# Opening of a two-block transformer kernel: x loaded ahead of the vectors, side loads behind it, zeros multiplied while TensorE waits

## The reference, cut to what matters

```python
def ada_mod(c, w, b, n):
    h = jax.nn.silu(c) @ w + b
    return jnp.split(h[:, None, :], n, axis=-1)

def gmlp_layer(x, c, ada_w, ada_b, norm_g, w_in, sgu_g, w_s, b_s, w_out):
    shift, scale, gate = ada_mod(c, ada_w, ada_b, 3)
    h = rms_norm(x, norm_g) * (1 + scale) + shift
    u, v, z = jnp.split(h @ w_in, 3, axis=-1)
    u = jax.nn.gelu(u)
    v = rms_norm(jax.nn.gelu(v), sgu_g)
    w_causal = jnp.tril(w_s)
    mixed = jnp.einsum('gts,bcsge->bctge', w_causal, v) + b_s
    y = u * mixed.reshape(bsz, s, A_WIDTH) * jax.nn.silu(z)
    return x + gate * (y @ w_out)
```

## Time and profile before

| | value |
|---|---|
| median of 3 runs | 1493.45 us (1486.89 to 1493.67) |
| the profiled execution | 1486.86 us |
| its span, first to last instruction | 1485.1 us |
| mean granted TensorE clock, share of full | 0.996 |
| TensorE busy | 1447.9 us, 97% |
| VectorE busy | 953.3 us, 64% |
| ScalarE busy | 624.3 us, 42% |
| DMA moved | 181.06 MB, 122 GB/s over the span |

### The profile page before, as it was taken

One profiled execution on the slowest core, in us unless ns is written; L12 is line 12 of the kernel. 1 busy time (PEld: TensorE's weight loads), 2 busy tenths in 40 slices (PEclk: granted clock), 3 DMA queues, 4 the chain that ended last, 5 costly groups with the idle time before them and its releaser, 6 DMA issues.

```text
span 1485.1 us, 19595 instructions
## 1 busy us (share of the span) xinstructions
PE 1447.9 (97%) x7404; PEld 1183.0 (80%) x7404; DVE 953.3 (64%) x1392; ACT 624.3 (42%) x916; POOL 124.8 (8%) x58
## 2 busy tenths in 40 slices
PE   5999999999999999999999999999899999999999
PEld 3998888888788688888877787777488888888887
DVE  5975777777888466666666868779777344332333
ACT  4734223332466444444444456655555232211221
POOL 0000100001100322222212100000020000000000
PEclk9999999999999999999999999999999999999999
DMA  9785544467622111111111232012021322222222
GB/s 378 302 344 201 185 183 170 169 242 284 265 75 86 61 63 51 56 55 56 57 57 57 85 115 86 29 60 84 1 102 70 113 85 103 95 98 101 85 92 78
DMA packets 34269, 181.06 MB, mean 122 GB/s; under 512 B 3865, under 2 KB 4121, under 8 KB 19618
## 3 DMA queue, kind: packets, MB, share of 16 engines
q1 hardware_dynamic: 32114, 175.22, 32.0%
q10 hardware_dynamic: 2096, 5.04, 1.0%
HBM read 178.14 MB, written 2.11 MB: 121 GB/s over the span
## 4 chain that ended last, share of the span: by engine, by line
PE 87%; DVE 6%; DMA 4%; issue 1%; ACT 1%; SPq 0%; ACTq 0%; DVEq 0%
PE acc L1519 75%; PE ada L1519 4%; PE norm L1519 4%; DMA ada_out<-in_ada 3%; PE turn L1519 2%; PE turn L1754 1%; DVE w_lo L915 1%; PE turn L1873 1%; DVE hx L908 1%; DMA wf_raw<-in_forget 1%; DVE hk_lo L908 0%; DVE s L908 0%; DVE ada_out L908 0%; DVE h_lo L908 0%; DVE stat L1373 0%
## 5 line engine op out<-in xcount | busy, mean ns | idle before, releaser
L1519 PE MATMUL acc<-h_hi,w_hi 128*128 128x512 f32 x984 | 400.8, 407 | 0.0
L1519 PE MATMUL acc<-h_hi,w_lo 128*128 128x512 f32 x984 | 383.8, 390 | 0.0
L1519 PE MATMUL acc<-h_lo,w_hi 128*128 128x512 f32 x984 | 383.5, 390 | 0.0
L915 DVE TENSOR_TENSOR w_lo<-w_raw,w_hi 128x2048 fp32r<-128x2048 f32 (+1 forms) x89 | 205.9, 2314 | 69.0 <-ACT w_hi L491 68.8
L491 ACT ACTIVATE w_hi<-w_raw 128x2048 fp32r<-128x2048 f32 (+1 forms) x106 | 200.7, 1893 | 117.1 <-PE acc L1519 117.0
L1519 PEld LDWEIGHTS acc<-h_hi,w_hi 128*128 128x128 f32 x984 | 184.9, 188 | 46.1 <-issue 9.0
L1519 PEld LDWEIGHTS acc<-h_lo,w_hi 128*128 128x128 f32 x984 | 185.0, 188 | 44.6 <-issue 8.1
L1519 PEld LDWEIGHTS acc<-h_hi,w_lo 128*128 128x128 f32 x984 | 184.7, 188 | 39.1
L445 POOL TENSOR_TENSOR w_lo<-w_raw,w_hi 128x2048 fp32r<-128x2048 f32 x17 | 77.3, 4548 | 322.4 <-ACT w_hi L491 322.4
L1519 PE MATMUL acc<-w_hi,h_hi 128*128 128x256 f32 x320 | 92.6, 289 | 0.0
L1519 PE MATMUL acc<-w_lo,h_hi 128*128 128x256 f32 x320 | 90.5, 283 | 0.0
(11 more groups left out here) (256 smaller groups left out, 2574.7 us busy)
## 6 DMA issues: line engine op xcount, KB each, us to landing
w_raw<-in_weights SPq DMA_DIRECT2D x102, 1024.0 KB, 4.7
ada_v<-in_ada SPq DMA_DIRECT2D x32, 512.0 KB, 5.9
ada_raw<-in_ada SPq DMA_DIRECT2D x32, 512.0 KB, 6.0
ada_out<-in_ada SPq DMA_DIRECT2D x32, 512.0 KB, 6.4
ada_up<-in_ada_first SPq DMA_DIRECT2D x8, 1024.0 KB, 20.2
w_raw<-in_weights SPq DMA_DIRECT2D x4, 768.0 KB, 4.2
x<-in_x SPq DMA_DIRECT2D x2, 1024.0 KB, 9.4
w_first<-in_weights SPq DMA_DIRECT2D x2, 1024.0 KB, 16.3
```

What stands on the lines that cost most here:

```text
L915: nc.vector.tensor_tensor(w_lo[par][:, 0:used], w_raw[par][:, 0:used], f32(w_hi[par][:, 0:used]), ALU.subtract)\
L1519: return nc.tensor.matmul(out, lhsT, rhs, start=start, stop=stop)
```

## The change

- SP issues the two halves of x right after c, and `vecs` behind them.
- The constants are laid out anew so that the matrix of ones and the epsilon are the first 132 columns. ACT issues just these first (`ones_loaded`). `csil[1]`, the rest of `consts`, and `ws_t` are issued in the loop over the tiles, after `h_hi` of tile 6; `lam_rows`, `bf_col`, `wf_raw` and `b_sp` after the loop.
- The load of the logarithm table moves from before the eight squares to behind them.
- DVE adds the squares in pairs (0+1, 2+3, 4+5, 6+7), ahead of the six gains, and TensorE adds the four sums with four products into `norm`.
- TensorE multiplies zeros into the bank `ada`: 6 products of 128 x 512 after spreading c, 16 after the sum of the squares. POOL clears the tile of zeros.
- `lam` moves: its two sums on DVE come after the masking of `ws_t`, behind a wait for all four small loads; its exponential on ACT after the statistics of v; `neg_lam` on DVE after them too. The wait for `small_loaded` ahead of the next stage goes.
- The third chunk's first group of tokens takes its 16 products with `h_hi` first and the 8 with `h_lo` behind them, one tile at a time as `h_lo` gets ready (`rows_late`). The wait for all of `h_lo` ahead of `v_pair(1)` goes, and `v_pair(1)` is taken out of the loop.

```diff
-    tiles = [ident, ones, half, causal_t, np.where(d >= 0, d, FAR), np.where(i >= j, 0.0, -FAR), slopes, last]
+    tiles = [ones, last, ident, half, causal_t, np.where(d >= 0, d, FAR), np.where(i >= j, 0.0, -FAR), slopes]
...
+    idle = at("idle", [P, TOK], T[7], F32R)
...
             sp.dma_start(c_in[:, :], d["c"]).then_inc(c_loaded, 16)
-            sp.dma_start(vecs[:, :], d["vecs"]).then_inc(vecs_loaded, 16)
             for half in range(2):
                 sp.dma_start(x[:, 4 * half:4 * half + 4, :], d["x"][:, 4 * half:4 * half + 4, :]).then_inc(x_loaded[half], 16)
+            sp.dma_start(vecs[:, :], d["vecs"]).then_inc(vecs_loaded, 16)
...
             nc.gpsimd.memset(one_row[:, :], 1.0).then_inc(one_ready, 1)
+            nc.gpsimd.memset(idle[:, :].bitcast(F32), 0.0).then_inc(idle_ready, 1)
...
-            act.dma_start(consts[:, :], d["tiles"]).then_inc(consts_loaded, 16)
-            act.dma_start(lam_rows[:, :], d["diff_lam_2"][0].rearrange("a b -> (a b)").partition_broadcast(P)).then_inc(small_loaded, 16)
-            act.dma_start(bf_col[:, :], d["b_f_2"].rearrange("a h -> h a")).then_inc(small_loaded, 16)
-            act.dma_start(wf_raw[:, :, :], d["forget"]).then_inc(small_loaded, 16)
-
-            act.dma_start(csil[1][:, :], d["c_2"][0].partition_broadcast(P)).then_inc(c2_loaded, 16)
+            act.dma_start(consts[:, 0:K_ID], d["tiles"][:, 0:K_ID]).then_inc(ones_loaded, 16)
...
-            act.preload_act_table_set("natural_log_exp_and_others")
             for kt in range(KT):
                 act.wait_ge(x_loaded[kt // 4], 16)
                 nc.scalar.activation(sq_first[kt][:, :], x[:, kt, :], ACT.Square).then_inc(sq_ready, 1)
+            act.preload_act_table_set("natural_log_exp_and_others")
             rstd_start(N_X0, NB[:, :], DM)
-            act.wait_ge(lam_part, 2)
-            nc.scalar.activation(lam_two[:, :], lam_two[:, :], ACT.Exp).then_inc(lam_exp, 1)
...
                 nc.scalar.activation(h_hi[:, kt, :], h_full[:, kt, :], ACT.Copy).then_inc(hhi_done, 1)
-
-            act.dma_start(ws_t[:, :, :], d["spatial"]).then_inc(ws_loaded, 16)
+                if kt == KT - 2:
+                    act.dma_start(csil[1][:, :], d["c_2"][0].partition_broadcast(P)).then_inc(c2_loaded, 16)
+                    act.dma_start(consts[:, K_ID:NCONST], d["tiles"][:, K_ID:NCONST]).then_inc(consts_loaded, 16)
+                    act.dma_start(ws_t[:, :, :], d["spatial"]).then_inc(ws_loaded, 16)
+
+            act.dma_start(lam_rows[:, :], d["diff_lam_2"][0].rearrange("a b -> (a b)").partition_broadcast(P)).then_inc(small_loaded, 16)
+            act.dma_start(bf_col[:, :], d["b_f_2"].rearrange("a h -> h a")).then_inc(small_loaded, 16)
+            act.dma_start(wf_raw[:, :, :], d["forget"]).then_inc(small_loaded, 16)
...
+            for i in range(KT // 2):
+                dve.wait_ge(sq_ready, 2 * i + 2)
+                nc.vector.tensor_tensor(sq_first[2 * i][:, :], sq_first[2 * i][:, :], sq_first[2 * i + 1][:, :], ALU.add)\
+                    .then_inc(sq_added, 1 + i // 2)
...
-            dve.wait_ge(small_loaded, 48)
-            for n in range(2):
-                stt(lam_prod[:, 64 * n:64 * n + 64], lam_rows[:, 128 * n:128 * n + 64], 1.0,
-                    lam_rows[:, 128 * n + 64:128 * n + 128], ALU.mult, ALU.mult, accum_out=lam_two[:, n:n + 1]).then_inc(lam_part, 1)
-            for m in range(1, KT - 1):
-                dve.wait_ge(sq_ready, m + 1)
-                if m > 1:
-                    dve.wait_ge(sq_added, m - 1)
-                nc.vector.tensor_tensor(sq_first[0][:, :], sq_first[0][:, :], sq_first[m][:, :], ALU.add).then_inc(sq_added, 1)
...
             nc.vector.tensor_tensor(ws_t[:, :, :], ws_t[:, :, :], tri, ALU.mult).then_inc(ws_ready, 1)
+            dve.wait_ge(small_loaded, 64)
+            for n in range(2):
+                stt(lam_prod[:, 64 * n:64 * n + 64], lam_rows[:, 128 * n:128 * n + 64], 1.0,
+                    lam_rows[:, 128 * n + 64:128 * n + 128], ALU.mult, ALU.mult, accum_out=lam_two[:, n:n + 1]).then_inc(lam_part, 1)
...
+            def stay_busy(n):
+                for _ in range(n):
+                    mm(AD[:, :], idle[:, 0:P], idle[:, :], True, True)
+
...
-            pe.wait_ge(consts_loaded, 16)
-            pe.wait_ge(sq_added, KT - 2)
-            mm(NB[:, :], ones, sq_first[0][:, :], True, False)
-            pe.wait_ge(sq_ready, KT)
-            mm(NB[:, :], ones, sq_first[KT - 1][:, :], False, True).then_inc(sum_done, 1)
+            pe.wait_ge(idle_ready, 1)
+            stay_busy(6)
+            pe.wait_ge(ones_loaded, 16)
+            for i in range(KT // 2):
+                pe.wait_ge(sq_added, (1, 2, 4, 6)[i])
+                last = mm(NB[:, :], ones, sq_first[2 * i][:, :], i == 0, i == KT // 2 - 1)
+            last.then_inc(sum_done, 1)
+            stay_busy(16)
...
+                            if first and (par, hb, t) == (0, 0, 0):
+                                last = rows_late(G[0][:, 0:256], 0, 0, 256)
...
-            h_ready(0, KT - 1)
-            with pe.Fori(1, W_UZ // 2) as u:
+            def rows_late(out, par, t, n):
+
+                wh = w_hi[par][:, :].rearrange("p (k n) -> p k n", k=KT)
+                wl = w_lo[par][:, :].rearrange("p (k n) -> p k n", k=KT)
+                s = slice(P * t, P * t + P)
+                for kt in range(KT):
+                    mm(out, h_hi[:, kt, s], wh[:, kt, 0:n], kt == 0, False)
+                    mm(out, h_hi[:, kt, s], wl[:, kt, 0:n], False, False)
+                for kt in range(KT):
+                    h_ready(0, kt)
+                    last = mm(out, h_lo[:, kt, s], wh[:, kt, 0:n], False, kt == KT - 1)
+                return last
+
+            v_pair(1, True)
+            with pe.Fori(2, W_UZ // 2) as u:
                 v_pair(u)
```

More of the change, by code:

```diff
@@ L100, in constants @@
     last = np.broadcast_to(np.array([EPS, 0.0, 0.0, 0.0]), (P, 4))
-    tiles = [ident, ones, half, causal_t, np.where(d >= 0, d, FAR), np.where(i >= j, 0.0, -FAR), slopes, last]
+    tiles = [ones, last, ident, half, causal_t, np.where(d >= 0, d, FAR), np.where(i >= j, 0.0, -FAR), slopes]
     return [np.concatenate(part, axis=1).astype(np.float32) for part in (tiles, blocks)]
-K_ID, K_ONE, K_HALF, K_TRI, K_DIST, K_MASK = 0, P, 2 * P, 3 * P, 4 * P, 4 * P + TOK
+K_ONE, K_EPS, K_ID = 0, P, P + 4
+K_HALF, K_TRI, K_DIST = K_ID + P, K_ID + 2 * P, K_ID + 3 * P
+K_MASK = K_DIST + TOK
 K_SLOPE = K_MASK + P
-K_EPS = K_SLOPE + 24
-NCONST = K_EPS + 4
+NCONST = K_SLOPE + 24
 def program(nc, d):
@@ L251, in sem @@
         return nc.alloc_semaphore(name)
-    vecs_loaded, consts_loaded, ws_loaded = sem("vecs_loaded"), sem("consts_loaded"), sem("ws_loaded")
+    vecs_loaded, ones_loaded, consts_loaded, ws_loaded = sem("vecs_loaded"), sem("ones_loaded"), sem("consts_loaded"), sem("ws_loaded")
     x_loaded = [sem("x_loaded0"), sem("x_loaded1")]
@@ L263, in program @@
     up_done, up_out, gsa_done = sem("up_done"), sem("up_out"), sem("gsa_done")
-    xn_done, one_ready = sem("xn_done"), sem("one_ready")
+    xn_done, one_ready, idle_ready = sem("xn_done"), sem("one_ready"), sem("idle_ready")
     hi_done, lo_done = sem("hi_done"), sem("lo_done")
@@ L597, in _ @@
             nc.scalar.activation(v_stat[:, 3, :], v_stat[:, 2, :], ACT.Square, scale=math.sqrt(0.5 / AW)).then_inc(v_stat_act, 1)
+            act.wait_ge(lam_part, 2)
+            nc.scalar.activation(lam_two[:, :], lam_two[:, :], ACT.Exp).then_inc(lam_exp, 1)
             def uz_pair(u):
@@ L1076, in _ @@
                 nc.vector.tensor_tensor(h_lo[:, kt, :], h_full[:, kt, :], f32(h_hi[:, kt, :]), ALU.subtract).then_inc(hlo_done, 1)
-            dve.wait_ge(lam_exp, 1)
-            stt(neg_lam[:, :], lam_two[:, 1:2], -LAM_INIT, lam_two[:, 0:1], ALU.add, ALU.subtract).then_inc(lam_ready, 1)
             ada_v_units(0, 0)
@@ L1101, in _ @@
             stt(v_stat[:, 5, :], v_stat[:, 4, :], 1.5, v_stat[:, 2, :], ALU.subtract, ALU.mult, reverse0=True).then_inc(v_stat_dve, 1)
+            dve.wait_ge(lam_exp, 1)
+            stt(neg_lam[:, :], lam_two[:, 1:2], -LAM_INIT, lam_two[:, 0:1], ALU.add, ALU.subtract).then_inc(lam_ready, 1)
             def uz_pair(u, cond):
@@ L1126, in uz_pair @@
                                             ALU.subtract).then_inc(ylo_done, 1)
-            dve.wait_ge(small_loaded, 64)
             half_uz = W_UZ // 2 + (C2_UNIT - FIRST_UZ_UNIT) // (2 * UNITS_UZ)
@@ L1603, in _, with v_pair @@
                 mm(G[n][:, :], one_row[:, :], c_in[:, TOK * n:TOK * n + TOK], True, True).then_inc(c_spread_in, 1)
-            pe.wait_ge(consts_loaded, 16)
-            pe.wait_ge(sq_added, KT - 2)
-            mm(NB[:, :], ones, sq_first[0][:, :], True, False)
-            pe.wait_ge(sq_ready, KT)
-            mm(NB[:, :], ones, sq_first[KT - 1][:, :], False, True).then_inc(sum_done, 1)
-            def v_pair(u):
-                n = 2 * u - W_V
+            pe.wait_ge(idle_ready, 1)
```

(7 more changed lines are left out.)

## The result

The changed kernel takes 1481.78 us (median of 20 runs, 1478.32 to 1486.60) against 1490.15 (20 runs of the kernel before, 1486.27 to 1493.67). The ratio is 0.9946, 95% interval 0.9936 to 0.9957: 8.0 us less, between 6.4 and 9.5. The profiled execution took 1483.68 us, its span is 1481.9. The forecast was 1484, with 6.3 us less.

What follows compares the result with a forecast made beforehand. TensorE was taken as the bound (87% of the chain), so it must start earlier or wait less: third chunk 6.7 us earlier, less 0.4 at chunk (2,0), gives 6.3; 1490.2 - 6.3 = 1483.9, predicted 1484 us, range 1476 to 1491.

Steps and rivals of the forecast that it cites:

- x and the bytes ahead: Opening loads: with a start of 3.4 us at 418 GB/s, x's halves land at 6.1 and 8.6 us.
- The norm: Opening, after the squares: the last pair is added by 11.95 us and its product ends at 12.9.
- The second `ada_up` is late next: DVE's `up_unit(1)` waits for this load behind 6.5 MB; DVE's series moves from 24.93 to 19.2, 5.7 us earlier.
- TensorE waits behind tile 0: First chunks: tile 0 ends at 21.7 at full rate, tile 1 comes at 22.9, so TensorE waits 1.2 us.
- Issues on ACT's path: ACT after tile 6: three DMA issues cost 1.35 us, later ones about 1.4; third chunk starts at 48.5.
- Low halves last: Third chunk: `h_lo` ends at 50.3, needed at 50.4; `rows_late` avoids a wait of 1.8 us, leaving none or 0.2.
- Chunk (2,0): Two chunks after the third chunk's start: its slack of 1.1 us is overdrawn by 0.3 to 0.4 us.
- The gain stays: Stages after chunk (2,0): TensorE or loads released by its own progress set the pace, so 6.3 us remains.
- E: Rival, later stages: the gain gets lost in a stage that loads pace; time 1486.9 us; chance 0.10.
- B: Rival, opening: products of zeros don't raise TensorE's clock; gain 4.0 us, time 1482.9; chance 0.15.
- D: Rival, DVE's wait for four small loads: late `b_sp` makes it slower, 1491 us if landing at 75; chance 0.05.
- C: Rival, opening: small loads and issues cost nothing, `ada_up` in time; gain about 8 us, time 1478.8; chance 0.15.

Runs made afterwards that it cites:

- side loads in front: Changed kernel with `csil[1]`, the rest of `consts`, `lam_rows`, `bf_col` and `wf_raw` issued at the start again, behind the ones; ratio 0.9980 to the kernel before.
- zeros alone: Kernel before with only the 22 products of zeros added; ratio 1.0002 to the kernel before.
- six zeros: Changed kernel without the 16 products of zeros behind the norm, keeping the 6 ahead of it; ratio 0.9952 to the kernel before.
- loads only: Changed kernel without any products of zeros and with the old third chunk, waiting for all eight `h_lo`; ratio 0.9967 to the kernel before.
- wait for all low halves: Changed kernel with the wait for all eight `h_lo` ahead of the third chunk and the old product order; ratio 0.9966 to the kernel before.

## Why the prediction was right, and where it was off

The time (1484 for 1481.78) and the sign came out; the size was a little too small (6.3 us, just below the interval of 6.4 to 9.5 around 8.0). Part of this is luck. The level that 6.3 was taken from, 1490.2, was the middle between two pairs of runs, a guess, and the median of before came out at 1490.15. And two misses partly cancel: the third chunk began 8.1 us earlier and not 6.7, and 1.0 us of it was lost ahead of chunk (2,0) and not 0.4. By its steps:

- *x and the bytes ahead.* Squares ran unbroken from 6.59 to 11.04; the sum had 6.8 to 11.2. The start of 3.4 us was the right end. Its reason is not shown: with the side loads in front again the second `ada_up`, behind 7.7 MB, fits a start of about 4.9 us, although the stretch at 116 GB/s isn't there.
- *The norm.* Ended at 13.4, not 12.9: its first products ran at half rate (1.06 to 1.08 each) and only those from 11 on at full rate (0.59). Harmless, since the load was later.
- *The second `ada_up` is late next.* Landed at 18.99, `up_unit(1)` at 19.01; the sum said 19.2 and not the 17.9 of the norm alone. (That 17.9 was 0.3 too late: `up_unit(1)` began 4.74 us behind the end of the norm, at 24.93 for 20.19, which from 12.9 gives 17.6. It bound nothing.) With 1.2 MB more in front it was 23.35, where the same sum would say 22.1.
- *TensorE waits behind tile 0.* 0.4 us instead of 1.2, as tile 0 began later (18.6) and tile 1 came sooner (22.7).
- *Issues on ACT's path.* This term was mis-sized. Three issues were priced at 1.35 us and kept ACT idle for 0.73 and DVE, ahead of `to_lo(1, 0)`, for 0.97; four at the end were priced to bring the table to 46.2 to 46.6, and it was loaded at 44.99. The step that was off is the sum of issue times: the first issue behind an activation runs beside it. So bank G[0] was empty in time and the third chunk began at 47.09 instead of 48.5.
- *Low halves last.* They ended at 49.5 (50.3 said), and there was no wait. Undone, the wait is 2.7 us, not 1.8, as TensorE is free at 47.0 and not at 48.5, and the cost at chunk (2,0) is 2.9: the clock that falls in the wait was left out.
- *Chunk (2,0).* The overdrawn slack was there: 0.8 us of waiting where 0.3 to 0.4 were said, larger because TensorE was earlier. The 0.38 us for `lam` fell into the wait for `ada_v`, still 1.12 us long behind them.
- *The gain stays.* 7.17 us at 84.50 and the same at 316.27. E fell; that the profiled spans differ by less is the clock, since TensorE's later waits are the same.
- *B*, zeros that give no clock, fell by the run with zeros alone and the one with six. The rule cited from the Trainium skill, "TensorE: Matmul & The Clock Gate" (The HAM clock gate), that activity releases the throttle, agrees with the traces for zeros as well: 0.67 and 0.59 a pair at 1.00 granted, against 1.19 at 0.50 without them. With the zeros alone the stretch from 18 to 22 us is at 0.50 and that from 24 to 26 at 1.00, and from 22 to 24, where the clock rose, TensorE multiplied nothing but zeros.
- *D.* `small_loaded` held nobody: `lam_prod` ran at 62.3, straight behind the masking.
- *C* was right in one half: the issues cost less than forecast. Its numbers were nearer than those of the forecast (third chunk at 46.7 to 47 for 47.09, gain of about 8 for 8.0), though `ada_up` was not in time as it said; its time of 1478.8 was taken from the profiled run and is that of the fastest runs only.

## What to carry to other kernels

In an opening, list what each engine waits for once the named wait is gone; here the load issued eighth on SP's queue decided. The bytes ahead of it, divided by the rate of the DMA engines, gave its landing to 0.2 us with a start of 3.4 us, but missed by more than 1 us once other loads stood in front, so such a sum needs a range. Keeping TensorE's clock up with products of zeros pays only as far as the next wait lets TensorE use the time, and if it makes TensorE wait longer, the clock can be lost there instead. Spread DMA issues behind activations in place of one block ahead of a table load.

## What the hardware showed unasked

- TensorE's granted clock fell in a wait of 2.7 us ahead of the third chunk, and in one of 5.2 ahead of tile 0; it did not in waits of 1.5 (changed kernel), 1.2 (loads only), 1.7 (zeros alone) and 2.5 us (side loads in front). After a fall, products ran at half rate for 3.0 (wait for all low halves) to 6.1 us (six zeros). The length of one wait doesn't decide it alone: of the dips in the later stages of the changed kernel, those between 1050 and 1075 us lie where TensorE's waits are 1.9 us at most, and those around 410 and 1130 where none is over 0.4.
- The profile shows a granted clock of 1.00 from the start, while the first products of every run took 1.05 to 1.08 us (float32 passes of 512 columns) where the same passes took 0.59 later. From this it looks as if the length of the rows tells the clock there, and not the column.
- The spread of runs, 8 us, goes with dips of the clock, in the traces mostly in the later stages: mean clock 0.998 to 0.999 in the runs of 1478 to 1479 us, 0.993 in those of 1486 to 1487. No edit of the opening touches those stages, and a single pair of profiles had 4 of the 7 us covered by them.
- The squares after silu needed no table load: ACT went from silu at 6.09 to the squares at 6.59.
